# A hybrid block and two attention layers: scores on both rings of PSUM banks, selection behind the evictions, a fused mask, more evictions on ScalarE

## The reference

```python
h = rms_norm(x, attn_norm_w); proj = h @ w_in
mixed = concat([retention_mixer(ret_cols), dsa_mixer(dsa_cols), dilated_mixer(dil_cols)])
x = x + mixed @ w_out
h = rms_norm(x, mlp_norm_w); x = x + square(relu(h @ w_up)) @ w_down
```

## Time and profile before

| | us |
|---|---|
| median of 3 runs | 1247.22 |
| the profiled execution | 1249.16 |
| its span, first to last instruction | 1247.9 |
| PE busy | 1198.4 (96%) |
| DVE busy | 760.6 (61%) |
| ACT busy | 669.1 (54%) |
| POOL busy | 345.4 (28%) |
| mean granted TensorE clock | 0.987 |

### The profile page before, as it was taken

One profiled execution on the slowest core, in us unless ns is written; L12 is line 12 of the kernel. 1 busy time (PEld: TensorE's weight loads), 2 busy tenths in 40 slices (PEclk: granted clock), 3 DMA queues, 4 the chain that ended last, 5 costly groups with the idle time before them and its releaser, 6 DMA issues.

```text
span 1247.9 us, 20494 instructions
## 1 busy us (share of the span) xinstructions
PE 1198.4 (96%) x8552; PEld 1107.6 (89%) x8552; DVE 760.6 (61%) x1026; ACT 669.1 (54%) x921; POOL 345.4 (28%) x117
## 2 busy tenths in 40 slices
PE   9798999999999999999899999999999999999997
PEld 8798999999989999999888789999899877999996
DVE  7878988687554655455677354544466763544444
ACT  5778776676435443435535864443454376634442
POOL 0000000025852211111554433222235453222221
PEclk9899999999999999999999999999999999999999
...
GB/s 300 148 135 146 226 203 170 203 137 169 190 147 236 202 193 179 197 175 128 177 138 99 102 141 203 196 193 180 160 190 157 136 102 102 196 193 190 183 200 34
DMA packets 152443, 210.77 MB, mean 169 GB/s; under 512 B 5504, under 2 KB 132640, under 8 KB 151712
## 3 DMA queue, kind: packets, MB, share of 16 engines
...
q10 hardware_dynamic: 768, 4.39, 0.9%
...
## 4 chain that ended last, share of the span: by engine, by line
PE 79%; DVE 10%; ACT 7%; issue 2%; DMA 1%; POOL 0%; SPq 0%; ACTq 0%; DVEq 0%
PE bank L516 78%; DVE w_lo L1354 2%; ACT tmp L970 2%; ACT w_hi L970 2%; PE bank L524 2%; DVE xbc L1362 1%; ACT L970 1%; DMA raw<-in_w_in 1%; DVE work L1728 1%; DVE keep L1749 1%; DVE top L1724 1%; DVE rk_t L1354 1%; ACT lru_ab L970 0%; ACT xbc L970 0%; DVE tmp L1354 0%
## 5 line engine op out<-in xcount | busy, mean ns | idle before, releaser
L516 PE MATMUL bank<-act_hi,w_hi 128*128 128x256 f32 (+1 forms) x2040 | 583.7, 288 | 18.1 <-DVE w_lo L1354 12.5
L516 PE MATMUL bank<-act_lo,w_hi 128*128 128x256 f32 (+1 forms) x2040 | 575.3, 284 | 0.0
L516 PE MATMUL bank<-act_hi,w_lo 128*128 128x256 f32 (+1 forms) x2040 | 565.1, 284 | 0.0
L1354 DVE TENSOR_TENSOR w_lo<-raw,w_hi 128x2048 fp32r<-128x2048 f32 (+4 forms) x174 | 369.1, 2122 | 238.7 <-ACT w_hi L970 238.7
L970 ACT ACTIVATE w_hi<-raw 128x2048 fp32r<-128x2048 f32 (+1 forms) x191 | 359.9, 1885 | 261.9 <-PE bank L516 259.2
L516 PEld LDWEIGHTS bank<-act_hi,w_hi 128*128 128x128 f32 (+1 forms) x2040 | 392.0, 192 | 28.2 <-issue 19.2
L516 PEld LDWEIGHTS bank<-act_lo,w_hi 128*128 128x128 f32 (+1 forms) x2040 | 392.4, 192 | 2.2 <-issue 0.5
L516 PEld LDWEIGHTS bank<-act_hi,w_lo 128*128 128x128 f32 (+1 forms) x2040 | 386.1, 192 | 0.0
L1927 POOL TENSOR_TENSOR w_lo<-raw,w_hi 128x1024 fp32r<-128x1024 f32 (+3 forms) x52 | 198.3, 3817 | 447.6 <-ACT w_hi L970 447.4
L1927 POOL TENSOR_TENSOR act_lo<-tmp,act_hi 128x512 fp32r<-128x512 f32 x52 | 135.9, 2617 | 433.8 <-ACT act_hi L970 433.8
L516 PE MATMUL bank<-w_hi,act_hi 128*128 128x512 f32 (+1 forms) x536 | 203.0, 379 | 6.8 <-DVE lq_t L1354 3.1
...
## 6 DMA issues: line engine op xcount, KB each, us to landing
...
```

The costliest lines, as they stand in the source:

```text
L516: return mm_ops.matmul(out, lhs, rhs, start=start, stop=stop, skip_group_check=True)
L1354: return ops.tensor_tensor(out, a, b, op)
```

## The change

1. **Banks.** `ret_s`, `ret_var` of the first pair of heads and all scores, transposes and value products of `att` are taken from `high`. Only the dsa scores of head 0 come from `low`, where `ret_o`, the means and `ret_var` of the second pair stay.
2. **Selection.** `sel_top` goes from mid to after the same tile. `sel_need` goes from mid dil_v 0 to after dil_q 0, `sel_keep` from mid dil_k 1 to after dil_v 0. `att dsa 0` goes from mid dil_q 1 to mid dil_k 1.
3. **Mask and scales.** The last three operations of `sel_keep` become two. The scale by rstd of the retention keys moves from the evacuation of ret_k into the decay product, now scalar_tensor_tensor.
4. **Evictions.** ACT evacuates qi and ret_k with a plain copy in place of DVE's product with rstd; the second column of `rstd_tok` holds rstd squared for the index score.
5. **ACT order.** In `att` steps 3 and 5 the copy of a finished output (`act_hi`) stands ahead of the normalization of the next heads.
6. **Opening of layer 0.** A square root of a constant ahead of the splits draws its table load forward. The split of dsa_q goes between the two roots on ACT, and on DVE ahead of the scaling of the residual.
7. **POOL.** `out` and `dsa_q` lose their share of 5/8, DVE does 2048 columns there. All other `w_lo` shares of POOL are issued in pieces of 512 columns.

The core of the diff:

```diff
+POOL_PIECE = 512
-POOL_SHARE = {"out_ssm": 4, "out_lru": 4, "out": 5,
-              "dsa_q": 5, "ret_k": 5, ...
+POOL_SHARE = {"out_ssm": 4, "out_lru": 4,
+              "ret_k": 5, ...
-        put("mid", ("dil_k", 2 * l), ("ret", l, 0, 0), ("sel_top", l, 2))
-        put("mid", ("dil_q", 2 * l), ("ret", l, 0, 1), ("ret", l, 1, 0), ("sel_top", l, 3))
+        put("mid", ("dil_k", 2 * l), ("ret", l, 0, 0))
+        put("after", ("dil_k", 2 * l), ("sel_top", l, 2))
+        put("mid", ("dil_q", 2 * l), ("ret", l, 0, 1), ("ret", l, 1, 0))
+        put("after", ("dil_q", 2 * l), ("sel_top", l, 3), ("sel_need", l))
...
@@ PE, ret and att
-                        bank = take(low, ("ret_s", s), at("ret_m", s + 1))
+                        bank = take(high, ("ret_s", s), at("ret_m", s + 1))
-                    bank = take(low, ("ret_var", n), at("ret_root", n + 1))
+                    bank = take(low if ch else high, ("ret_var", n), at("ret_root", n + 1))
-                ring = high if dilated or (step >= 2) else low
-                        bank = take(ring, (a, "s", s), at(f"{a}_p", s + 1))
+                        bank = take(low if a == "dsa" and h == 0 else high, (a, "s", s), at(f"{a}_p", s + 1))
@@ ACT, evac
+                if name in ("qi", "ret_k"):
+                    act.wait_ge(*used(name, j))
+                    dst = qi_t[:, 2 * (j % 2):2 * (j % 2) + 2, :] if name == "qi" else rk_t[:, :, :]
+                    fn(dst, pair(bank), ACT.Copy).then_inc(*tick(name))
@@ ACT, opening of layer 0 (n == 1)
+                    fn(cols[:, 31:32], eps[:, :], ACT.Sqrt)
                     lead(T["qi", 1] - LEAD)
...
+                    lead(T["dsa_q", 0] - LEAD)
@@ DVE, sel_keep
-                tt(more[:, :], more[:, :], eq[:, :], ALU.add).then_inc(*tick("dve_step"))
+                stt(more[:, :], more[:, :], -1.0, eq[:, :], ALU.add, ALU.add).then_inc(*tick("dve_step"))
-                ts(more[:, :], more[:, :], -1.0, ALU.add, -MASKED, ALU.mult).then_inc(*tick("dve_step"))
-                tt(keep[:, :], more[:, :], c["causal"], ALU.min).then_inc(*tick("keep"))
+                stt(keep[:, :], more[:, :], -MASKED, c["causal"], ALU.mult, ALU.min).then_inc(*tick("keep"))
@@ DVE, ret step 0
-                        tt(m[:, 0:SEQ], bank[:, 0:SEQ], dec, ALU.mult)
+                        stt(m[:, 0:SEQ], bank[:, 0:SEQ], rstd_tok[:, 0:1], dec, ALU.mult, ALU.mult)
@@ POOL, lead
+                    for c0 in range(0, cuts[n], POOL_PIECE):
+                        s = slice(c0, min(c0 + POOL_PIECE, cuts[n]))
+                        inst = tt(lo[:, s], src[:, s], hi[:, s].bitcast(F32), ALU.subtract)
+                    inst.then_inc(*tick("w_lo_pool"))
```

More of the change, by code:

```diff
@@ L128 @@
 TOKENS = ("ret_v", "dil_v")
-POOL_SHARE = {"out_ssm": 4, "out_lru": 4, "out": 5,
-              "dsa_q": 5, "ret_k": 5, "ret_q": 5, "ret_v": 5, "ret_g": 5, "dil_k": 7, "dil_q": 7, "dil_v": 8,
+POOL_SHARE = {"out_ssm": 4, "out_lru": 4,
+              "ret_k": 5, "ret_q": 5, "ret_v": 5, "ret_g": 5, "dil_k": 7, "dil_q": 7, "dil_v": 8,
               "out_2": 8}
@@ L906, in att @@
                         s = 4 * l + h - heads[0]
-                        bank = take(ring, (a, "t", s), at(f"{a}_pt", s + 1))
+                        bank = take(high, (a, "t", s), at(f"{a}_pt", s + 1))
                         pe.wait_ge(*at(f"{a}_n", s + 1))
@@ L913, in att @@
                     n = 2 * l + step // 2 - 1
-                    bank = take(ring, (a, "o", n), at(f"{a}_lo", n + 1))
+                    bank = take(high, (a, "o", n), at(f"{a}_lo", n + 1))
                     pe.wait_ge(*at(f"{a}_pt", 2 * n + 2))
@@ L1249, in att @@
                         inst.then_inc(*tick(f"{a}_e"))
+                if step in (3, 5):
+                    n = 2 * l + step // 2 - 1
+                    k = chunk0 + heads[step - 3] // 2
+                    act.wait_ge(*at(f"{a}_o", n + 1))
+                    act.wait_ge(*(used("down", 12 + k // 2) if l else used("ffn_out", (8, 9, 10, 7)[k // 2])))
+                    fn(act_hi[:, k, :], psum[a, "o", n][:, 0:SEQ], ACT.Copy).then_inc(*tick(f"{a}_hi"))
                 if step in (1, 3):
@@ L1404, in evac @@
                 bank = psum.get((name, j))
-                if name not in DOWNS and name not in TOKENS:
+                if name not in DOWNS and name not in TOKENS and name not in ("qi", "ret_k"):
                     vec.wait_ge(*used(name, j))
@@ L1453, in evac @@
                     inst.then_inc(*tick("ki"))
-                if name in ("qi", "dsa_q", "ret_k", "ret_q", "ret_g", "dil_k", "dil_q"):
+                if name in ("dsa_q", "ret_q", "ret_g", "dil_k", "dil_q"):
                     k = 2 * (j % 2)
-                    dst, kind = {"qi": (qi_t[:, k:k + 2, :], "qi"), "dsa_q": (dq_t[:, :, :], "dq"),
-                                 "ret_k": (rk_t[:, :, :], "ret_k"), "ret_q": (rq_t[:, :, :], "ret_q"),
+                    dst, kind = {"dsa_q": (dq_t[:, :, :], "dq"), "ret_q": (rq_t[:, :, :], "ret_q"),
                                  "ret_g": (rg_t[:, :, :], "rg_raw"), "dil_k": (lk_t[:, k:k + 2, :], "dil_k"),
@@ L1780, in ret @@
                         vec.wait_ge(*at("ret_o", n))
[L1781 to L1782 removed]
+                        stt(m[:, 0:SEQ], bank[:, 0:SEQ], rstd_tok[:, 0:1], dec, ALU.mult, ALU.mult)
+                        stt(m[:, SEQ:KQ], bank[:, SEQ:KQ], rstd_tok[:, 1:2], dec[:, 0:P], ALU.mult, ALU.mult).then_inc(
+                            *tick("ret_m"))
                 if step == 1:
```

27 lines of the change are left out of this document (10 added, 17 removed).

## The result

| | before | changed |
|---|---|---|
| median, us | 1247.26 (4 runs, 1247.18 to 1249.12) | 1235.67 (4 runs, 1234.26 to 1237.20) |
| profiled execution, us | 1249.16 | 1235.14 |
| its span, us | 1247.9 | 1233.8 |
| PE idle in the span, us | 49.5 | 42.3 |
| mean granted clock | 0.987 | 0.993 |

The ratio is 0.9901, 95% interval 0.9886 to 0.9917. The change makes the kernel faster by 11.6 us, clear of the noise but half of the 23.5 forecast, and the time lies above the stated range of 1219.5 to 1233.

What follows compares the result with a forecast made beforehand. PE was taken as the limit, busy 1198.4 of 1247.9 us, with its waits to save. Savings 22 + 4.0 + 0.7 - 3.2 = 23.5 us took 1249.16 to 1225.7; less 1.94, the median was 1223.7, range 1219.5 to 1233.

Steps and rivals of the forecast that it cites:

- signs of being right: No PE wait over 1 us at three places, scans under 1.3, opening restart within about 1.1, PE idle down 15 to 18.
- Banks at dil_q 0 and the tiles dil_v: Bank waits for lk_t and lq_t go: 2.29 us plus 1.7 of clock, and 1.6 at dil_v, per layer.
- Selection at dil_q 1: The variance's wait for lk_t goes, as DVE writes it earlier: 2.03 us and 1.7 of clock per layer.
- ACT order: At out_2, the transpose's wait for act_lo behind an ACT normalization shrinks: 1.65 of 1.77 us per layer.
- Opening: Layer 0: PE restarts 2.3 us earlier, with 1.7 of clock: 4.0 us saved, bounds 1.5 and 4.8.
- Tile out: First block: DVE does all 2048 columns itself and is not held up by POOL: 0.7 us saved, between 0 and 2.
- New waits: ACT's two added table loads and ret_k copy cost 0 to 3.16 us per layer; 1.6 taken, 3.2 in all.
- the first rival: Tie count's tensor_scalars held behind POOL pieces, DVE some 3 us later: 4.5 per layer, 1232.7 us; chance 0.2.
- the two tiles of lead: POOL's pieces: four take 5.1 us instead of 4.60; splits running two tiles ahead hide the 0.5 us.
- The second, waits that move: PE meets the next late thing at each place; clock parts and half the lengths come back: 1230.3 us; chance 0.17.
- The third, POOL's pieces holding DVE: Attention tiles: DVE held at piece boundaries up to 1.27 us each; slower, 1261.8 us at fifteen holds per layer; chance 0.03.
- the forecast's case: All savings come, less the new waits: median 1223.7 us, own range 1219.5 to 1227; chance 0.55.

Runs made afterwards that it cites:

- rings_only: The kernel before with only the change's bank rings (part 1): 1250.86 us, ratio 1.0024 to the kernel before.
- sel_only: The kernel before with only the selection stages moved as in the change, on the old rings, dsa scores left in dil_q 1: 1237.84 us, ratio 0.9908.
- combo_oldrings: combo on the old rings of banks: 1225.09 us, ratio 0.9805 to the kernel before.
- combo_actorder: combo with ACT's copy of a finished output (act_hi) behind the normalization again, as before the change: 1223.15 us, ratio 0.9795.
- one_piece: The changed kernel with POOL's subtractions whole again (POOL_PIECE 2048 in place of 512): 1232.22 us, ratio 0.9869 to the kernel before.
- dsa_back: The changed kernel with the first dsa scores back in dil_q 1 from dil_k 1: 1232.06 us, ratio 0.9863 to the kernel before.
- need_late: The changed kernel with the tie count (sel_need) after dil_v 0 in place of after dil_q 0: 1232.24 us, ratio 0.9865 to the kernel before.
- lo_first: The changed kernel with POOL's second low part of retention's output issued ahead of the split of out_2's second tile: 1227.74 us, ratio 0.9830.
- combo: The changed kernel with lo_first, need_late, dsa_back and POOL's subtractions whole only in out_ssm and out_lru: 1220.58 us, ratio 0.9771 to the kernel before.

## Why the prediction was wrong

Nearly every saving was right in place and size. Of the signs of being right named ahead, the three places have no wait over 1 us, the scans took 1.00 and the opening 0.96; but PE's idle time fell by 7.2 us, not 15 to 18. Behind each term is what the profile after shows.

- Banks at dil_q 0 and the tiles dil_v: the waits of 2.29, 0.78 and 0.79 are gone in both layers, with the clock. The reason given was half right: rings_only shows that the rings remove the 2.29, but sel_only and combo_oldrings that the order on DVE is enough for it, and only the 1.6 per layer needs the rings.
- Selection at dil_q 1: the wait of 2.03 is gone. The two scans took 1.00 us in the changed kernel, 0.9 was forecast.
- ACT order: 1.77 is gone; 1.65 was forecast, and combo_actorder brings 1.71 back.
- Opening: from the row at 592.50 (593.09 after) to PE's restart it was 9.80 us and is 7.38, so 2.4 against 2.3, and the wait is 0.96 against 1.1 forecast. The clock of that stretch is 1.00. No run takes apart what the opening's four edits bring, so their shares are the forecast's alone.
- Tile out: PE's wait there went from 2.79 to 2.09, 0.7 as forecast, and it is 2.09 in one_piece too, where PE does not come late from the 1.04 us at 329.46.

**The step that failed is "New waits".** It took 1.6 us per layer, between 0 and 3.16, from ACT's added work alone. The profile has 1.30 + 1.01 + 2.78 = 5.09 per layer, beyond the upper bound, and 1.65 of clock behind the last in one layer. Each part has a run of its own, in us of waits per layer:

- ACT's added work: 1.67 go with it (dsa_back). This is the term as priced, 1.6.
- The tie count held beside POOL: the 1.30 for `lv` (need_late). The sum had it at nothing, since it was left to the first rival.
- The order on POOL, the small `act_lo` behind the split: 2.77 + 0.27 - 0.65 = 2.4 (lo_first). The prediction had it nowhere.

The three make 5.4, and combo, which has all three edits, has 5.1 us less of waits per layer than the changed kernel. So the parts add nearly as they are. With the term failed the sentence that POOL's pieces are hidden by the two tiles of lead: in these traces no wait of PE in the attention tiles is for POOL's `w_lo`, but one is for the small `act_lo` queued behind it, and there is one in the first block, where POOL works on the low parts of activations as well (1.04 us at 329.46). The account: 2 x (5.09 - 1.6) + 1.04 + 1.65 = 9.7, against 23.5 - 14.0 = 9.5 us that the profiled execution missed. The medians add 2.5: the forecast took off the 1.94 by which the profiled execution of before was above its median, and the one after was 0.53 below. With the three edits the savings arrive: combo has 1220.58, where the forecast without its new waits would be 1223.7 - 3.2 = 1220.5. That the two agree to 0.1 us is luck, as the groups alone differ by more.

What had been to see: POOL's row at 695.07 in the kernel before ended 0.26 us before PE started. When PE is to come several us earlier, a slack of 0.26 us is a wait, unless its producer comes earlier by as much. PE was there at 685.87, 10.2 us earlier, and `act_lo` was ready at 688.51, 7.3 us earlier. The two added table loads on ACT are the smaller part of that: without them the wait is still 2.12 (dsa_back). The order on POOL made it costly: with that alone changed the wait is gone and the median 1227.74 (lo_first).

**The rivals.** The first, the tie count held up, happened: 4.01 in place of 1.00 us, where "some 3 us later" was said. It cost 1.30 per layer and no clock, against the 4.5 priced. It had been given 0.2, as the forecast excluded it. On the rule quoted there from the Trainium skill ("SBUF — State Buffer", section "Who interferes with whom"), that tensor_scalar can contend with GpSimd and is then blocked for whole instructions, the traces agree: four took 1.00 us with POOL idle, 4.01 beside pieces, and a single one 3.14 beside a whole subtraction. The second, waits that move, happened as well, and rings_only is its pure case. It had ACT's results and the transposes in it, but not POOL's queue. It left 3.8 us of waits per layer, and 1.01 + 2.78 = 3.79 came; this match is luck, since 3.8 was half of what was saved and most of the 2.78 is the order on POOL. The third, POOL's pieces holding DVE, did not decide: with whole subtractions the kernel was no slower (one_piece). What pieces cost PE, 1.04 us at 329.46 and 0.4 per layer at out_2, came by POOL being late and not DVE.

So the forecast's case, the first rival and the second were held as exclusive with a chance each, where parts of all came at once. Adding the rivals' extra costs by their chances would have helped little: 0.2 x 9.0 + 0.17 x 6.6 + 0.03 x 38 = 4.1 us, to 1227.8. At their measured size the new waits are 2 x 5.09 = 10.2 us, of which the forecast had 3.2. The other 7.0 needed POOL's queue in the list, and no rival had it.

What stays open: why the clock falls behind a wait of 2.8 us in one execution and not in another. The runs show that it does, not what decides it. The last 1 us of lo_first's gain has no row. What the fused mask, ACT's evictions and the pieces bring each by themselves on the kernel before was not run.
